# Neighbourhood attention with grid rows ordered by columns, and two heads at a time on halves of TensorE's array

## The chip, the cores and the metric

The kernel runs on one core of a Trainium2 chip. The time is the device time of one execution in microseconds (us), the median of several runs. A profile of one further execution gives the instructions of each engine: TensorE (PE, with its weight loads as PEld), VectorE (DVE), ScalarE (ACT), GpSimd (POOL) and SyncE (SP), the last of which mainly issues DMA transfers here.

## The reference, cut to what matters

Two transformer blocks in float32 over 512 tokens of width 1024. The first has neighbourhood attention beside a convolution branch, then a mixture of experts; the second has two kinds of causal attention and a layer of retrieved experts. Only the attention of the first block is changed. Its 512 tokens are a grid of 8 rows and 64 columns. A query sees all 8 rows, but only a window of 16 columns, and besides that 256 context keys:

```python
cq = jnp.arange(GRID_W)[:, None]                       # GRID_W = 64
ck = jnp.arange(GRID_W)[None, :]
c_start = jnp.clip(cq - WIN_COLS // 2, 0, GRID_W - WIN_COLS)   # WIN_COLS = 16
col_mask = (ck >= c_start) & (ck < c_start + WIN_COLS)
...
s_loc = einsum('bhqd,bhkd->bhqk', q_r, k_blk) * scale + bias   # bias from rpb by row and column distance
s_loc = jnp.where(band_mask, s_loc, NEG_INF)
s_ctx = einsum('bhqd,bhkd->bhqk', q_r, k_ctx) * scale
p = jax.nn.softmax(jnp.concatenate([s_loc, s_ctx], axis=-1), axis=-1)
return einsum('bhqk,bhkd->bhqd', p[..., :n_loc], v_blk) + einsum('bhqk,bhkd->bhqd', p[..., n_loc:], v_ctx)
```

## The kernel before

The program is one block of code per engine. Each engine runs its instructions in order, and semaphores (`wait_ge`, `then_inc`) tie the engines together; the order of the work is written out by hand. Almost every vector and scalar instruction goes through `link`, which also waits for its own end.

**Start.** SP loads four 2 MB slabs of `w_mod`, then the context and x (L620, L621). Rows are normalised, transposed on TensorE (L1884) and scaled into `hT` by ScalarE (L892, L895). Then TensorE makes the GLU inputs of the convolution (L1846), VectorE the product `u_pad` (L1377) and the depthwise convolution (L1382), while TensorE makes k, v and q: 18 projections, copied out by ScalarE (q at L917).

**Slabs.** All weights pass through a ring of six slots. SP issues slab n when slab n - 6 has been read (L618). Slabs 9 to 28 belong to five modulation jobs of four slabs each (the function `modulation`, L1861), slabs 29 to 34 to the merge.

**The attention loop** takes 32 units n, one head and 128 queries each. TensorE at step n: `scores(n)` (L1940: 512 local keys, L1941: 256 context keys, contraction over the 64 channels of the head), `transposes(n - 2)` (L1950: six 128x128 tiles), `weighted(n - 3)` (L1963: six products of 64x128 into one half of bank 6). VectorE adds the bias (with the window's mask in it) and takes the maximum (L1420), takes that of the context scores (L1422), joins them (L1423), then normalises unit n - 1 (L1406 to L1408). ScalarE makes the exponentials (L956, L958) and copies the transposed weights of unit n - 2 to SBUF (L944, L946), and at the end of a head its output (L952). Between the steps stand two sums of the convolution's layer norm (`conv_mean` L1903, `conv_var` L1909; on VectorE `conv_centre` and `conv_norm`), and at n = 6, 11, 16, 21 (`AT_JOB`) modulation jobs 1 to 4. A job writes four rows, on partitions 0, 32, 64 and 96; VectorE adds the bias to each (L1367), POOL stores them (L777). Job 0 runs among the projections.

**The bias.** POOL writes a table `skew_d`, 64 copies of each padded row of `rpb` (L768, four transfers, 3.9 MB), and reads from it for each head, with a skewed pattern in pieces of 256 bytes, a [128, 14, 64] bias (L795). These loads are spread over the loop, each behind the maxima of an earlier head.

**Merge.** For each of eight c TensorE computes two gates and two branch products (L1846), ScalarE the sigmoids (L978, L979), VectorE `mixT` (L1439 to L1441). Then `w_o`, the second norm and the experts.

## Time and profile before

| what | us |
|---|---|
| median of 3 runs | 3176.17 (3174.83 to 3188.65) |
| the profiled execution, whole | 3168.23 |
| its span, first to last instruction | 3166.5 |
| TensorE busy in the span | 2314.8 |
| VectorE busy | 1449.2 |
| ScalarE busy | 730.2 |

The span is what the views are dated in, from its first instruction. Busy time is a union over the instructions of an engine: matmuls overlap, so the mean duration of a record is longer than the pace at which records follow each other. A float32 product leaves two matmul records and a transpose one. Share of busy time says little by itself; what counts is which engine or transfer ends last at each place.

### The profile page before, as it was taken

The numbers are of one execution on the slowest core, as the hardware profiler recorded it, in microseconds if no ns is written. First come the engines' busy times: TensorE is split into PE (matmuls) and PEld (weight loads), VectorE is DVE, ScalarE is ACT, GpSimd is POOL, SyncE is SP. The second block draws the span as 40 slices with busy tenths as digits, with TensorE's granted clock in tenths as the row PEclk, the third lists the DMA queues.
The fourth block names the chain that finished last, engine by engine and source line by source line (L and its number), as shares of the span: only waits on it lengthen the run. The fifth ranks groups of instructions, "written<-read, shape, count | busy, mean of one in ns | idle before, by whom it ended". The sixth has DMA issues, their size and how long they took to land.

```text
span 3166.5 us, 29164 instructions
## 1 busy us (share of the span) xinstructions
PE 2314.8 (73%) x9846; PEld 1013.0 (32%) x9846; DVE 1449.2 (46%) x3427; ACT 730.2 (23%) x1764; POOL 615.8 (19%) x604
## 2 busy tenths in 40 slices
PE   2998999976787777299886887646775656565554
PEld 1444554442222222154465643312221111111110
DVE  1295431141000000300138766756777777777775
ACT  2004430011000000221225543312222322232222
POOL 1000100001000000100001222234444443444442
PEclk8999999977999899699788788777787777777777
DMA  7416833826999999621125777789999999999996
GB/s 258 167 54 217 289 115 109 258 98 263 405 405 404 406 406 402 215 102 53 54 73 205 282 292 278 291 338 394 416 418 421 421 421 421 421 412 421 422 421 278
DMA packets 218493, 928.24 MB, mean 293 GB/s; under 512 B 19385, under 2 KB 59384, under 8 KB 127486
## 3 DMA queue, kind: packets, MB, share of 16 engines
q0 software_dynamic: 80752, 558.26, 43.5%
q1 hardware_dynamic: 127824, 359.68, 30.7%
q10 hardware_dynamic: 9790, 8.73, 0.8%
q8 instruction: 66, 1.08, 0.1%
q14 instruction: 61, 0.50, 0.0%
HBM read 891.42 MB, written 35.18 MB: 293 GB/s over the span
## 4 chain that ended last, share of the span: by engine, by line
DMA 29%; PE 26%; DVE 12%; issue 5%; ACT 4%; POOL 1%; SPq 0%; DVEq 0%; POOLq 0%; ACTq 0%
DMA ring<-in_expert_pair,ids 14%; DMA ring<-in_w_exp_up 11%; PE bank L1846 7%; PE bank L2052 5%; PE bank L2370 4%; DVE ring L1795 4%; PE bank L1852 4%; DMA arena_v<-in_expert_pair,ids 2%; DMA pair_last<-in_expert_pair,ids 2%; PE bank L2383 1%; ACT arena_w L1248 1%; DMA ring<-in_w_exp_down 1%; POOL ring L852 1%; PE bank L2185 1%; PE bank L2186 1%
## 5 line engine op out<-in xcount | busy, mean ns | idle before, releaser
L2370 PE MATMUL bank<-ring,arena_w 128*32 128x512 f32 x1568 | 546.9, 818 | 356.0 <-ACT arena_w L1248 353.4
L852 POOL DMA_INDIRECT ring<-in_expert_pair,ids x392 | 423.4, 1080 | 1118.3 <-PE bank L2370 661.1
L1846 PE MATMUL bank<-arena_h,ring 128*128 128x512 f32 (+1 forms) x1024 | 373.2, 525 | 12.1 <-DMA ring<-in_w_in 10.0
L2052 PE MATMUL bank<-ring,arena_h 128*64 128x512 f32 x1056 | 278.7, 688 | 82.8 <-DMA ring<-in_w_exp_up 74.6
L2370 PEld LDWEIGHTS bank<-ring,arena_w 128*32 128x32 f32 x1568 | 94.3, 131 | 670.7 <-ACT arena_w L1248 502.1
L1795 DVE CUSTOM_DVE_ANT_0 ring<-ring,arena_h 128x1024 f32<-128x1024 f32 x203 | 245.8, 1226 | 114.6 <-DMA ring<-in_expert_pair,ids 82.6
L1795 DVE CUSTOM_DVE_ANT_0 ring<-ring 128x1024 f32<-128x1024 f32 x189 | 229.7, 1225 | 76.9 <-DMA ring<-in_expert_pair,ids 67.6
L1846 PEld LDWEIGHTS bank<-arena_h,ring 128*128 128x128 f32 x1024 | 178.8, 196 | 195.8 <-issue 192.8
L1541 DVE TENSOR_TENSOR arena_q<-arena_q,bank 128x256 f32<-128x256 f32 x32 | 13.5, 421 | 494.5 <-ACT arena_q L1016 494.5
L1246 ACT ACTIVATE arena_w<-arena_w 128x2 f32<-128x2 f32 (+1 forms) x224 | 45.4, 203 | 763.1 <-DVE arena_w L1795 762.9
L2052 PEld LDWEIGHTS bank<-ring,arena_h 128*64 128x64 f32 x1056 | 96.5, 157 | 263.5 <-issue 254.7
L2370 PE MATMUL bank<-pair_last,arena_w 128*32 128x512 f32 x200 | 134.4, 810 | 25.3 <-ACT arena_w L1248 25.3
L2065 PE MATMUL bank<-ring,arena_q 128*64 128x512 f32 x528 | 120.6, 598 | 19.8 <-DVE arena_q L1544 19.3
L1248 ACT ACTIVATE arena_w<-arena_w 128x32 f32<-128x32 f32 x512 | 132.9, 312 | 7.3
L2370 PE MATMUL bank<-arena_h,arena_w 128*32 128x512 f32 x140 | 96.2, 826 | 38.4 <-ACT arena_w L1248 38.4
L833 POOL DMA_INDIRECT arena_v<-ys_d,slot_i x8 | 8.0, 1004 | 574.4 <-SPq L682 564.2
L2370 PE MATMUL bank<-arena_v,arena_w 128*32 128x512 f32 x140 | 94.9, 816 | 33.0 <-ACT arena_w L1248 33.0
L1852 PE MATMUL bank<-ring,arena_h 128*128 128x512 f32 x224 | 100.7, 609 | 1.0 <-ACT arena_h L1192 0.8
L1382 DVE SCALAR_TENSOR_TENSOR arena_x<-arena_x,convc 128x512 f32<-128x512 f32 x120 | 90.2, 752 | 4.3
L1016 ACT ACTIVATE arena_q<-bank 128x256 f32<-128x256 f32 x32 | 12.3, 384 | 321.3 <-PE bank L2052 321.3
L1852 PE MATMUL bank<-ring,arena_q 128*128 128x512 f32 x176 | 78.0, 603 | 3.6 <-DVE arena_q L1441 3.6
L1439 DVE TENSOR_TENSOR arena_w<-bank,arena_w 128x512 f32<-128x512 f32 x8 | 5.5, 692 | 159.8 <-ACT arena_w L979 159.8
(465 smaller groups left out, 3248.5 us busy)
## 6 DMA issues: line engine op xcount, KB each, us to landing
ring<-in_w_exp_gate SPq DMA_DIRECT2D x33, 2048.0 KB, 19.8
ring<-in_w_exp_up SPq DMA_DIRECT2D x33, 2048.0 KB, 24.2
ring<-in_w_exp_down SPq DMA_DIRECT2D x33, 2048.0 KB, 25.0
ring<-in_w_in SPq DMA_DIRECT2D x15, 2048.0 KB, 22.8
ring<-in_w_mod SPq DMA_DIRECT2D x12, 2048.0 KB, 9.7
ring<-in_w_ada SPq DMA_DIRECT2D x12, 2048.0 KB, 18.3
xs_d<-zeros SPq DMA_DIRECT2D x1, 12032.0 KB, 69.4
arena_h<-xs_d SPq DMA_DIRECT2D x66, 128.0 KB, 23.2
```

The costliest lines, as they stand in the source:

```text
L852: pool.indirect_dma_start(pair[pair_of(m)], None, A["expert_pair_2"], bass.IndirectOffsetOnAxis(ap=ids[n % 2][:, r:r + 1], axis=0)).then_i ...
L1246: link(act.activation(gel[:, k0:k0 + count], dots[:, k0:k0 + count], ACT.Gelu))
L1248: act.activation(sel_q[:, n % 2, k, :], sel_q[:, n % 2, k, :], ACT.Copy, scale=gel[:, k:k + 1]).then_inc(sel_done, 1)
L1382: link(dve.scalar_tensor_tensor(out=conv[:, cc, :], in0=u_pad[:, cc, k:k + T], scalar=convc[:, cc, k:k + 1], in1=conv[:, cc, :], op0=ALU.m ...
L1795: dve.tensor_tensor_reduce(buf, buf, h2_q[r % 4], 1.0, 0.0, ALU.mult, ALU.add, dots[:, r:r + 1]).then_inc(dots_done, 1)
L1846: mm = pe.matmul(dst, w[:, c, at], rhs[:, c, :], start=(c == 0), stop=(c == chunks - 1))
L1852: mm = pe.matmul(dst, xT[:, c, t * P:(t + 1) * P], w[:, c, at], start=(c == 0), stop=(c == chunks - 1))
L2052: mm = pe.matmul(bank[2 + b][at, :].rearrange("p (g f) -> p g f", g=2), xbT[b][:, c, :], gu[:, :, c, 256 * half:256 * half + 256], start=( ...
L2065: mm = pe.matmul(bank[6 + b][CAP * j:CAP * j + CAP, :], hidT[b][:, k, CAP * half:CAP * half + CAP], slab(n)[:, half, k, 512 * j:512 * j + ...
L2185: pe.matmul(dst[:, 0:w], fqT[at, h // 2, t * P:(t + 1) * P], fkT[at, h // 2, 0:w], start=True, stop=False)
L2186: pe.matmul(dst[:, 0:w], ident[0:H, h:h + 1].broadcast_to([H, P]), fcumT[:, 0:w], start=False, stop=False)
L2370: mm = pe.matmul(bank[4 + 2 * (n // H % 2) + half][at, :], sel_q[:, n % 2, k0 + j, :], pair[pair_of(m + j)][:, D + 512 * half:D + 512 * ha ...
```

## The change

Tokens are held column by column in the first block's attention: position 8 c + r for grid column c and row r. A group of 128 queries (16 columns; q is rotated by 64 positions, that is 8 columns) then sees only 256 neighbouring keys, and the fourth group, made of the two edges, 128 each. x is loaded in that order by eight transfers, one per grid row. The convolution needs the order by rows, so `u_pad` is written, and the gates of the merge are written, through a permuted view (`by_columns`, `in_rows`).

The loop takes 16 units i (`PU`), each two heads and 128 queries. The heads of a pair sit on the two halves of the partitions, and `scores` and `weighted` alternate between them, on row halves and on column halves of the array. Local and context scores share one bank, so one maximum and one exponential per head do. VectorE adds the bias in the bank itself. The division of a unit's work is:

| per pair of heads and 128 queries | before | after |
|---|---|---|
| score products, columns | 4: 2 x 512, 2 x 256 | 4 x 256 |
| transposes | 12 | 8 (6 in every fourth) |
| weighted products of 128 columns | 12 | 8 |

The bias table becomes 23 copies of 120 rows of 48 floats, written in one transfer in pieces of 192 bytes; a pair's bias is read in pieces of 1536 bytes into `rpb_raw`, and VectorE makes the bias with the mask from it (`bias_of`). Jobs use a stationary operand of 32 equal columns in place of one, so that VectorE adds all 128 partitions in one instruction. The jobs move to steps 4, 8, 11 and 14 of 16. `probT` takes the space of `pair_last`. The core of the diff:

```diff
-        PROJ_JOB, AT_MEAN, AT_VAR, AT_JOB = 10, 1, 4, (6, 11, 16, 21)
+        PROJ_JOB, AT_MEAN, AT_VAR, AT_JOB = 10, 0, 2, (4, 8, 11, 14)
...
-                    sp.dma_start(xr, A["x"].rearrange("(t p) d -> p t d", p=P)).then_inc(x_in, 16)
+                    for r in range(ROWS):
+                        sp.dma_start(xr[r:P:ROWS, :, :], A["x"][r * GRID_W:(r + 1) * GRID_W, :].rearrange("(t c) d -> c t d", t=TT))\
+                            .then_inc(x_in, 16)
...
+            pool.dma_start(skew_d[:, :, :].rearrange("i n w -> n i w"),
+                           rpb_pad[0:H * RPB_R, :].unsqueeze(1).broadcast_to([H * RPB_R, COPIES, SKEW])).then_inc(skew_out, 16)
...
+            def bias_rows(hp):
+
+                if hp >= 1:
+                    pool.wait_ge(nmax_done, 8 * (hp - 1) + 1)
+                for e in range(2):
+                    at = skew.offset + ((2 * hp + e) * RPB_R + ROWS - 1) * SKEW + WIN - 1
+                    pool.dma_start(rpb_raw[:, e, :], bass.AP(skew.tensor, at, [[copy - 1, WIN], [copy - SKEW, ROWS], [1, ROWS * SKEW]]))                        .then_inc(bias_in[hp % 2], 16)
+
+            bias_rows(0)
+            store_rows(0)
+            bias_rows(1)
+            store_rows(1)
+            bias_rows(2)
+            store_rows(2)
+            bias_rows(3)
+            store_rows(3)
+            store_rows(4)
...
-                    link(act.activation(qT[:, m - 14, :], src[:, :], ACT.Copy, scale=HD ** -0.5), proj_out)
+                    link(act.activation(qT[:, m - 14, 0:T - 64], src[:, 64:T], ACT.Copy, scale=HD ** -0.5))
+                    link(act.activation(qT[:, m - 14, T - 64:T], src[:, 0:64], ACT.Copy, scale=HD ** -0.5), proj_out)
...
+            def exps(i):
+                w = LOC[i % TT] + CTX
+                for e in range(2):
+                    m = 2 * i + e
+                    act.wait_ge(nmax_done, m + 1)
+                    if m >= 6:
+                        act.wait_ge(pT_done, m - 5)
+                    link(act.activation(prob[m % 6][:, 0:w], bank[2 * (i % 2) + e][:, 0:w], ACT.Exp, bias=neg_max(m),
+                                        accum_out=ssum[:, 0, m:m + 1]), p_done)
+
+            def probs_out(i):
+                w = LOC[i % TT] + CTX
+                for e in range(2):
+                    m = 2 * i + e
+                    act.wait_ge(pT_done, m + 1)
+                    if m >= 4:
+                        act.wait_ge(o_done, m - 3)
+                    link(act.activation(probT[m % 4][:, 0:w // P, :], bank[4 + e][:, 0:w].rearrange("p (a b) -> p a b", b=P), ACT.Copy), pTa_out)
...
-                for j in range(4):
-                    at = slice(32 * j, 32 * j + 1)
-                    link(dve.tensor_tensor(mod_row[at, :], bank[7 if i else 0][at, :], mod_bias[i % 3][at, :], ALU.add), mod_rows)
+                dve.tensor_tensor(mod_row, bank[7 if i else 0][:, :], mod_bias[i % 3], ALU.add).then_inc(mod_rows, 4)
...
-                link(dve.tensor_tensor(u_pad[:, cc, PADC:PADC + T], bank[2 * (cc % 2)][:, :], sig[cc % 2], ALU.mult), u_done)
+                link(dve.tensor_tensor(in_rows(u_pad[:, cc, PADC:PADC + T]), by_columns(bank[2 * (cc % 2)][:, :]),
+                                       by_columns(sig[cc % 2]), ALU.mult), u_done)
...
+            def maxima(i):
+                w = LOC[i % TT]
+                for e in range(2):
+                    m = 2 * i + e
+                    s, b = bank[2 * (i % 2) + e], bias[:, e, 0:256] if w == 256 else bias[:, e, 256:384]
+                    dve.wait_ge(s_done, m + 1)
+                    link(dve.tensor_tensor(s[:, 0:w], s[:, 0:w], b, ALU.add))
+                    link(dve.tensor_reduce(neg_max(m), s[:, 0:w + CTX], AX, ALU.max, negate=True), nmax_done)
+
+            def normalise(i):
+
+                for e in range(2):
+                    m = 2 * i + e
+                    dve.wait_ge(p_done, m + 1)
+                    one = slice(m % 4, m % 4 + 1)
+                    link(dve.reciprocal(rinv[:, one], ssum[:, 0, m:m + 1]))
+                    p = prob[m % 6][:, 0:LOC[i % TT] + CTX]
+                    link(dve.tensor_scalar(p, p, rinv[:, one], None, ALU.mult), pn_done)
...
+                            rows, v = 32, cvec[:, vecs, c:c + 1].broadcast_to([P, 32])
...
+            def scores(i):
+                hp, u = i // TT, i % TT
+                if i >= 2:
+                    pe.wait_ge(p_done, 2 * i - 2)
+                keys = ((u * P, 2 * P, 0, P),) if u < TT - 1 else ((T - P, P, 0, 64), (0, P, 64, 64))
+                for k0, width, q0, queries in keys:
+                    for e in range(2):
+                        pe.matmul(bank[2 * (i % 2) + e][q0:q0 + queries, 0:width], qT[halves(e), hp, u * P + q0:u * P + q0 + queries],
+                                  kT[halves(e), hp, k0:k0 + width], start=True, stop=True)
+                for e in range(2):
+                    pe.matmul(bank[2 * (i % 2) + e][:, LOC[u]:LOC[u] + CTX], qT[halves(e), hp, u * P:(u + 1) * P],
+                              kcT[halves(e), hp, :], start=True, stop=True).then_inc(s_done, 1)
+
+            def transposes(i):
+                for e in range(2):
+                    m = 2 * i + e
+                    pe.wait_ge(pn_done, m + 1)
+                    if m >= 2:
+                        pe.wait_ge(pTa_out, m - 1)
...
+                for k, (v, chunk, q0, queries) in enumerate(terms):
+                    for e in range(2):
+                        at = slice((2 * hp + e) * HD, (2 * hp + e + 1) * HD)
+                        mm = pe.matmul(bank[6][halves(e), u * P + q0:u * P + q0 + queries], v[:, at],
+                                       probT[(2 * i + e) % 4][:, chunk, q0:q0 + queries], start=(k == 0), stop=(k == len(terms) - 1))
```

## Rows read from the trace of the kernel before

**Rows 1.** The page, part 2: busy tenths of TensorE in 40 equal slices of the span.
```profile
PE   2998999976787777299886887646775656565554
```

**Rows 2.** Timeline of PE, 225 to 460: start, duration, engine, line, operation.
```profile
277.51 4.34 PE L1909 MATMUL bank<-arena_x,mean_w 128*128 128x512 f32 x8
289.81 7.05 PE L1861 MATMUL bank<-ring,cvec 128*1 128x512 f32 x64
...
381.98 7.05 PE L1861 MATMUL bank<-ring,cvec 128*1 128x512 f32 x64
440.44 14.00 PE L1846 MATMUL bank<-arena_h,ring 128*128 128x512 f32 x32 [0.74 <-ACT arena_v L952]
```

**Rows 3.** By stretch, busy: PE, PEld, DVE, ACT, POOL; then PEclk, DMA share, GB/s.
```profile
254.00:440.40 186.40, 166.07 (x976) 99.91 (x976) 104.08 (x261) 93.59 (x215) 19.95 (x31) 0.94 0.74 252
440.40:636.00 195.60, 191.95 (x443) 84.76 (x444) 20.75 (x30) 13.38 (x21) 4.01 (x7) 0.99 0.55 165
...
138.20:254.40 116.20, 115.57 (x349) 55.25 (x347) 96.23 (x129) 9.83 (x18) 2.01 (x4) 1.00 0.21 73
```

**Rows 4.** Timeline of one step, 398 to 414: PE and its weight loads.
```profile
403.84 0.88 PE L1950 MATMUL bank<-ident,spare 128*128 128x128 f32 x6
...
404.64 1.28 PEld L1963 LDWEIGHTS bank<-arena_w,arena_v 128*64 128x64 f32 x12 [0.17 <-issue]
...
406.10 1.12 PE L1940 MATMUL bank<-arena_q 64*128 64x512 f32 x2
...
407.06 0.59 PE L1941 MATMUL bank<-arena_v,arena_q 64*128 64x256 f32 x2
```

**Rows 5.** Chain that ended last: start, duration; expert products on 64-column halves.
```profile
757.22 6.89 PE bank L2052 x32
```

**Rows 6.** Groups by form, 254 to 441: busy us, mean ns, idle before.
```profile
L1408 DVE TENSOR_SCALAR arena_w<-arena_w,rinv 128x768 f32<-128x768 f32 x22 | 14.0, 635 | 0.8
L1422 DVE TENSOR_REDUCE smx<-bank 128x1 f32<-128x256 f32 x32 | 13.6, 424 | 1.1
...
L1407 DVE RECIPROCAL rinv<-rinv 128x1 f32<-128x1 f32 x32 | 5.3, 164 | 1.1
...
L1313 DVE RECIPROCAL arena_x<-arena_x 128x512 f32<-128x512 f32 x1 | 3.4, 3352 | 0.0
```

**Rows 7.** Groups by form, 0 to 1050: a 512-wide pass of VectorE from a bank.
```profile
L1439 DVE TENSOR_TENSOR arena_w<-bank,arena_w 128x512 f32<-128x512 f32 x8 | 5.5, 692 | 159.8 <-ACT arena_w L979 159.8
```

**Rows 8.** Line L618: three slab loads issued from 325 to 330, time to landing.
```profile
L618 SPq DMA_DIRECT2D ring<-in_w_ada x3: 540/667/3872, 327.8 to 329.1; - x3
DMA to landing us min/median/max: 9.8/14.6/19.3
```

**Rows 9.** Timeline of the start, by engine.
```profile
78.72 21.45 PE L1846 MATMUL bank<-arena_h,ring 128*128 128x512 f32 x43 [10.01 <-DMA ring<-in_w_in]
...
53.92 3.43 POOL L768 DMA_DIRECT2D skew_d<-arena_w  x3 [1.71 <-DMA arena_w<-in_rpb]
...
43.55 1.06 ACT L883 ACTIVATE arena_q<-arena_v 128x1024 f32<-128x1024 f32 x1 [24.67 <-DMA arena_x<-in_x]
...
64.69 6.46 ACT L895 ACTIVATE arena_h<-bank,mcol,acol 128x512 f32<-128x512 f32 x8
```

**Rows 10.** Line L618: three slab loads issued from 52 to 56, time to landing.
```profile
L618 SPq DMA_DIRECT2D ring<-in_w_in x3: 551/669/1631, 53.0 to 54.3; - x3
DMA to landing us min/median/max: 14.8/25.0/32.1
```

**Rows 11.** DMA, 84 to 100: rate in 40 slices; bias loads, size and landing.
```profile
GB/s 415 394 353 379 389 394 404 399 410 399 389 399 384 394 379 399 404 328 215 225 236 230 230 164 230 246 230 236 251 251 236 215 215 231 312 389 389 384 384 389
...
arena_w<-skew_d POOLq DMA_DIRECT2D x4, 224.0 KB, 8.5
```

**Rows 12.** By stretch of 3 us, columns as in rows 3.
```profile
303.00:306.00 3.00, 0.93 (x7) 0.79 (x8) 2.86 (x6) 1.83 (x6) 2.55 (x6) 1.00 1.00 354
306.00:309.00 3.00, 3.00 (x13) 2.51 (x13) 1.79 (x5) 2.26 (x6) 1.54 (x2) 0.52 1.05 393
```

242 lines of the change are left out of this document (101 added, 141 removed).

## The prediction

> **What bounds the kernel now.** Start from the page [rows 1]: slices 2 to 8 (79 to 633 us) hold TensorE at 80% and more, and the change touches only this front part, before the experts. Next the timeline of TensorE [rows 2] dates the stages: the attention loop ends at 440.4, where the merge of the branches begins. Inside it stand four modulation jobs of 7.05 us, the first at 289.8 and the last at 382.0, so 30.7 us apart, and two convolution sums of about 4 us (one stands in rows 2). The loop begins at 254.4, where the projections end [rows 3]. The table of stretches [rows 3] says what limits the loop: of 186.4 us TensorE is busy 166.1, VectorE 104.1, ScalarE 93.6, and the DMA engines 0.74 of the time. So the loop is TensorE's; VectorE and the weight stream are the next two floors. One steady step [rows 4] shows the order: transposes 403.84, weighted sums 404.64, scores 406.10 and 407.06, which end at 407.65. With the waits between about 4 us a step, in 32 steps.
>
> The merge waits for all of the loop, and after it TensorE is busy 191.95 of 195.6 us [rows 3]. The expert weights are loaded into slots that the merge frees, so the stages behind move with it. I carry a gain at 440 us through one for one.
>
> **Scores.** Before: per step a 64x512 and a 64x256 product, two records each; 1.56 us from 406.10 to the end at 407.65 [rows 4]; for a pair of heads 3.1. After: per pair of heads and 128 queries four products of 256 columns, eight records. A 512-column record costs 0.44 us back to back (14.00 us for 32) [rows 2], so a 256-column one 0.22. One behind another: 8 x 0.22 = 1.75. Two at a time: 0.9, with gaps 1.1. No row shows row halves at work together (the two heads there write two banks). The nearest rows are column pieces: the expert product on 64-column halves takes 6.89 us for 32 records, 0.215 each, and the modulation 7.05 us for 64, 0.11 each [rows 5, 2], against 0.44 whole [rows 2]. I take 1.1 and keep 1.75.
>
> **Transposes.** Six in 0.88 us, 0.145 each [rows 4]. From 12 to 8 per pair (6 in every fourth unit): 1.16 us.
>
> **Weighted sums.** 12 records of 128 columns in 1.46 us (404.64 to 406.10), 0.12 each [rows 4]; before, all of a head go to one half. Per pair from 24 to 16 alternating records: 2.0 us one behind another, 1.1 side by side. Here [rows 5] speaks directly for the halves, so 1.1.
>
> TensorE's step is 1.1 + 1.16 + 1.1 = 3.4 us. The Trainium skill ("TensorEngine Tiling (Array Packing)", Key Properties) says that a change of tiling mode drains TensorE, and each step has three changes. The trace shows 0.17 us at such a point (0.17 <-issue [rows 4]). By the page such drains stay, but there are 16 steps with them in place of 32; priced at the row it is 0.5 us a step, and 3.9 in place of 3.4.
>
> **VectorE.** Per head: an add of 256 from and to a bank (no row writes to a bank; the nearest pass from one is 424 ns for 256 [rows 6]), a maximum over 512 (692 for a 512-wide pass [rows 7]), a reciprocal of 0.164 and a scaling of 512 (0.635 for 768 [rows 6]; 0.42 in proportion, 0.49 with a fixed part). With 0.05 between links: 3.9 us per pair, 3.2 in every fourth unit, mean 3.7. Bounds: the bank write at 0.3 to twice 0.42, so 3.6 to 4.7. ScalarE, busy 93.6 us in the old loop [rows 3], has four passes of 512 per pair (two exponentials, two copies) where it had eight of 512 or 256, so it is not the bound. VectorE sets the step, about 3.9 us. Besides it keeps what it had: centring, four passes of 0.69; normalisation, a reciprocal of 3.35 and eight passes, about 9; and bias preparations, four of about 1.5 [rows 6, 7]. The rows of a job fall from four passes to one.
>
> **Jobs.** The same 64 products in 7.05 us; weight loads of 32 columns in place of 1. The expert products have loads of 64 columns and keep the full pace for two halves [rows 5], so such loads lie under products. Cost 0 to 1 us each; I take 0.
>
> **The weight stream.** This becomes the floor. Each job uses four 2 MB slabs and frees their four slots; the next job needs the first two of the batch issued then. After the second job the loads go out from 327.8 on and land 9.8, 14.6 and 19.3 us later [rows 8]: about 4.7 us of lead and 5.1 a slab, unless an earlier batch is still running. Job to job is thus at least 7.05 + 14.6 = 21.7 us, near the bandwidth floor of 4 x 5.1 = 20.4. Before, the interval was 30.7, and the stream had pauses (share 0.74 [rows 3]).
>
> **The loop, added up.** To job 1 (step 4): five steps, the two sums of 8 us, and the waits between sums and VectorE's centring and variance: about 25 us. By then job 1 has its slabs: three are issued as the projections end and land by 4.7 + 3 x 5.1 = 20 us. Job 1 to 2, four steps: VectorE has normalisation 9, about 4 x 3.9 of steps, a bias 1.5 and the rows 0.7: 27 us. Jobs 2 to 3 and 3 to 4, three steps each: 7 + 3 x 3.9 is 19, less than the 21.7 of the stream, so 22 each. After job 4: 7 us, then the remaining step and three draining ones, about 14 us; the merge's first four slabs, two of which are issued only after job 4, need 14.6. So 22. Sum 25 + 27 + 22 + 22 + 22 = 118, plus 2 for a dip of the clock: **120 us in place of 186, 66 less**.
>
> **The start.** TensorE stands still for 10 us until 78.7, when its second GLU slab lands (issued 53.6, 25.0 us) [rows 9, 10]. That slab shares the engines with the bias table's copies, three of 960 KB issued from 53.9 [rows 9]. After, the table is 2760 pieces of 192 bytes, 0.53 MB. Pieces of 256 bytes can be priced: from 91 to 97 us four loads of 224 KB (3584 pieces) pull the rate from about 395 to about 230 GB/s [rows 11]; own bytes and loss make some 1.9 MB, about 4.9 us, 1.4 ns a piece. So 2760 cost 3.8 us: the slab at 53.6 + 14.6 + 3.8 = 72. The inputs of the product are ready at 71.2 (64.69 + 6.46) [rows 9]. The stage starts at 72.2, **6.5 us earlier**, and stays TensorE-bound to 254 [rows 3], so the gain passes. Bounds 9 and -8 (writes five times as dear). Loading x in eight strided pieces in place of one: the bytes are the same, ScalarE began on them at 43.55 [rows 9], and a delay has 0.9 us of cover by the slab, which would land at 72. 0, at worst 3.
>
> **Covered.** The GLU's strided write has 14 us of products per piece (16 products of two records of 0.44). Two copies for one in q and at the heads' end: 0.2 each. The merge's strided sigmoids and product stand beside 24 us of products per turn (195.6 in eight [rows 3]); only the last turn shows, 0 to 2. POOL: each bias load now stands in front of a store of rows and is issued when the pair before has been read; none comes late. TensorE's in-order wait for a job's slabs now has scores queued behind it; VectorE waits for these, and that is in the 22s.
>
> **Sum.** 66 + 6.5 = 72.5 less than the 3168.2 us of the profiled execution: 3095.7. The runs' median is 8 us higher, so 3104.
>
> **Rivals.** (1) The halves do not run together (the change does not do what it says, as to time). For: no row has row halves in fp32. Against: [rows 5]. TensorE's step is 1.75 + 1.16 + 2.0 + 0.5 = 5.4: 16 x 5.4 + 28 + 8 + 8 = 130 us, 10 more: 3114. If only the rows fail, 3108. (2) The clock. With TensorE busy 0.93 of 3 us, the granted clock in the next 3 us is 0.52, the level of 1.2 GHz [rows 12]. The new loop has many short waits. With half of it at 1.2 GHz TensorE's steps average 5.1 and some jobs take 14: 15 us more, 3119; all of it, 31 more, 3135. The Trainium skill ("TensorE: Matmul & The Clock Gate", Loop structure matters more than you think) says that gaps between bursts let the clock fall; the trace agrees [rows 12], but the 0.94 over the loop says how seldom so far [rows 3]. (3) A larger gain: steps of 3.6, clean stream, 110 us and 9 at the start: 85 less, 3091. (4) Slower than before: the 192-byte writes. They share the engines with the GLU slabs; each ns a piece delays these by 2.8 us, so above 72.5 / 2.76 + 1.4 = 28 ns the whole gain is gone; at 40 the stage starts at 53.6 + 14.6 + 110 = 178, 106 after the 72.2 of the forecast: 3210. Against: 1.4 ns for the like read.
>
> **How the numbers follow.** Forecast 0.55, (1) 0.15, (2) 0.17, (3) 0.10, (4) 0.03. The range 3088 to 3138 takes in the first four. Half a percent (about what a measurement here tells from no change) is 16 us: faster 0.94, same 0.03, slower 0.03.
>
> **What would show it.** Right: the four jobs some 22 to 27 us apart, each ending a wait for a slab; TensorE's idle time ended by DMA in jobs 3 and 4; the expert-like 0.11 to 0.15 us per record in scores and sums; GLU products from about 72. Wrong: score records not overlapping, VectorE's add well over 0.42, a clock near 0.5 over long stretches, a late x, or a merge that begins well away from 367.

## The result, and the profile after

| what | us |
|---|---|
| median of before, 4 runs | 3175.5 (3169.76 to 3188.65) |
| median of after, 4 runs | 3129.05 (3124.04 to 3138.84) |
| ratio, with its 95% interval | 0.9852 (0.9812 to 0.9892) |
| the profiled execution of after, whole and span | 3138.84, 3137.0 |

The kernel is 46 us faster, 1.5%. The forecast was 72 us and 3104; the time lies in the range of 3088 to 3138, 25 us above the forecast. A second series of the same kernel (`a1_after_again`, below) gave 3128.31 and a ratio of 0.9811 (0.9765 to 0.9858). The profiled execution of after is the slowest of its four, so its span is only 29.5 us shorter than that of before (3166.5).

The timeline of TensorE of after, to be read against [rows 2] and [rows 9]. Columns: start, duration, engine, line, operation, tiles and number of records, and in brackets the idle time before it and what ended that. L1897 is a modulation job, L1944 the convolution's second sum, L1878 at 379.90 the first product of the merge. In the loop L1979 and L1982 are scores, L1992 transposes, L2006 weighted sums.

```profile
75.62 9.61 PE L1878 MATMUL bank<-arena_h,ring 128*128 128x512 f32 x18 [2.54 <-ACT arena_h L913]
...
251.60 3.70 PE L1938 MATMUL bank<-arena_x,mean_w 128*128 128x512 f32 x8
...
265.90 5.75 PE L1944 MATMUL bank<-arena_x,mean_w 128*128 128x512 f32 x8 [4.47 <-ACT arena_x L946]
...
278.32 7.07 PE L1897 MATMUL bank<-ring,cvec 128*32 128x512 f32 x64
285.32 0.70 PE L1979 MATMUL bank<-arena_q 64*128 64x256 f32 x4
285.86 0.60 PE L1982 MATMUL bank<-arena_v,arena_q 64*128 64x256 f32 x4
286.39 0.88 PE L1992 MATMUL bank<-ident,arena_w 128*128 128x128 f32 x6
287.19 1.09 PE L2006 MATMUL bank<-pair_last,arena_v 128*64 128x128 f32 x16
288.22 0.70 PE L1979 MATMUL bank<-arena_q 64*128 64x256 f32 x4
...
297.39 1.94 PE L1992 MATMUL bank<-ident,arena_w 128*128 128x128 f32 x8 [8.04 <-ACT pair_last L976]
...
307.48 7.07 PE L1897 MATMUL bank<-ring,cvec 128*32 128x512 f32 x64
...
331.02 8.77 PE L1897 MATMUL bank<-ring,cvec 128*32 128x512 f32 x64 [3.21 <-DMA ring<-in_w_ada]
...
355.28 8.77 PE L1897 MATMUL bank<-ring,cvec 128*32 128x512 f32 x64 [4.13 <-DMA ring<-in_w_ada]
...
379.90 15.36 PE L1878 MATMUL bank<-arena_h,ring 128*128 128x512 f32 x32 [6.58 <-DMA ring<-in_w_conv_out]
```

The merge starts at 379.90 in place of 440.44, so 60.5 us earlier. The mechanism of the forecast is in the last three rows: job 3, job 4 and the merge each stand behind a wait for a slab. Before job 2 there is no such wait; there TensorE waits 8.04 us for ScalarE's copy of earlier transposes. This copy stands behind the convolution's SiLU (L955) and the exponentials, and SiLU stands behind VectorE's normalisation. ScalarE's timeline of that stretch:

```profile
289.17 1.28 ACT L955 ACT_TABLE_LOAD   x1 [5.12 <-DVE arena_x L1421]
290.46 3.35 ACT L955 ACTIVATE arena_x<-arena_x,convc 128x512 f32<-128x512 f32 x4
293.84 1.28 ACT L966 ACT_TABLE_LOAD   x1
295.13 0.69 ACT L966 ACTIVATE arena_w<-bank,smx 128x512 f32<-128x512 f32 x1
...
296.75 1.01 ACT L976 ACTIVATE pair_last<-bank 128x384 f32<-128x384 f32 x2
```

VectorE's first maximum of the step is ready at 292.46 (291.77 + 0.69 in its timeline), and ScalarE's exponential on it starts only at 295.13, behind SiLU and its two table loads. A part of TensorE's step is read by starts: scores 285.32 to 286.39, 1.07 us; weighted sums 287.19 to 288.22, 1.03 us.

By stretch, the first row for the loop, the second for GLU and projections, as in [rows 3] (PE, PEld, DVE, ACT, POOL busy, then PEclk, DMA share, GB/s):

```profile
250.40:379.80 129.40, 93.72 (x792) 52.38 (x792) 74.07 (x155) 58.32 (x119) 14.27 (x28) 0.88 0.93 329
75.60:250.40 174.80, 173.97 (x480) 81.50 (x480) 98.98 (x132) 14.18 (x27) 2.10 (x4) 0.99 0.24 85
```

The loop has shrunk from 186.4 to 129.4 us. TensorE was busy 0.89 of it and is now busy 0.72; the DMA share has risen from 0.74 to 0.93, VectorE's part from 0.56 to 0.57. From job 2 on the loop belongs to the weight stream now. VectorE's groups by form in the loop (busy, mean ns, idle before), to be set against [rows 6, 7]:

```profile
L1440 DVE TENSOR_REDUCE smx<-bank 128x1 f32<-128x512 f32 x24 | 16.6, 691 | 0.8
L1450 DVE TENSOR_SCALAR arena_w<-arena_w,rinv 128x512 f32<-128x512 f32 x24 | 11.8, 492 | 0.8
L1439 DVE TENSOR_TENSOR bank<-bank,arena_w 128x256 f32<-128x256 f32 x24 | 10.3, 431 | 33.5 <-PE bank L1982 33.0
L1448 DVE RECIPROCAL rinv<-ssum 128x1 f32<-128x1 f32 x32 | 5.2, 163 | 1.1
```

Four durations, four hits: 0.691 for 0.69, 0.492 for 0.49, 0.431 for 0.42, 0.163 for 0.164. The 33.0 us of idle time ahead of the add are spent waiting for scores, so VectorE isn't the bound of the whole loop either.

### The profile page after: what moved, and what is told of

It reads as the page before. It is cut to its first block, busy times and chain, and to the rows that moved or that the text cites. A ratio compares the mean times of both kernels' runs of the same rounds, so it can differ in the third digit from the quotient of the medians.

```text
span 3137.0 us, 28550 instructions
## 1 busy us (share of the span) xinstructions
PE 2262.7 (72%) x9662; PEld 971.0 (31%) x9662; DVE 1419.5 (45%) x3317; ACT 703.2 (22%) x1672; POOL 603.3 (19%) x593
## 4 chain that ended last, share of the span: by engine, by line
DMA 32%; PE 27%; DVE 11%; issue 4%; ACT 4%; POOL 1%; SPq 0%; DVEq 0%; POOLq 0%; ACTq 0%
DMA ring<-in_expert_pair,ids 17%; DMA ring<-in_w_exp_up 11%; PE bank L1878 7%; PE bank L2097 5%; PE bank L2415 5%; DVE ring L1827 4%; PE bank L1884 3%; DMA arena_v<-in_expert_pair,ids 1%; POOL ring L870 1%; PE bank L2428 1%; ACT arena_w L1274 1%; DMA pair_last<-in_expert_pair,ids 1%; PE bank L2230 1%; DMA ring<-in_w_exp_down 1%; PE bank L2231 1%
## 5 line engine op out<-in xcount | busy, mean ns | idle before, releaser
L1878 PE MATMUL bank<-arena_h,ring 128*128 128x512 f32 (+1 forms) x1024 | 372.5, 524 | 10.5 <-DMA ring<-in_w_conv_out 6.6
L2097 PE MATMUL bank<-ring,arena_h 128*64 128x512 f32 x1056 | 282.7, 696 | 91.6 <-DMA ring<-in_w_exp_up 81.2
L1878 PEld LDWEIGHTS bank<-arena_h,ring 128*128 128x128 f32 x1024 | 178.6, 196 | 193.4 <-issue 188.7
L1878 PE MATMUL bank<-arena_q,ring 128*128 128x384 f32 x224 | 81.0, 524 | 0.0
## 6 DMA issues: line engine op xcount, KB each, us to landing
ring<-in_w_exp_up SPq DMA_DIRECT2D x33, 2048.0 KB, 24.8
```

The costliest lines, as they stand in the source:

```text
L1878: mm = pe.matmul(dst, w[:, c, at], rhs[:, c, :], start=(c == 0), stop=(c == chunks - 1))
L2097: mm = pe.matmul(bank[2 + b][at, :].rearrange("p (g f) -> p g f", g=2), xbT[b][:, c, :], gu[:, :, c, 256 * half:256 * half + 256], start=( ...
```

## Where 26 us of the forecast went

The sum forecast a merge 72.5 us earlier, and the rest carried through. Here is each stretch in several traces, dated by the first products of merge and experts, the last gate or up product of the experts, and the span. `before`, `b1` and `b2` have the attention of before; in `b2` x comes in eight transfers.

| stretch, us | before | b1 | b2 | after | a1 | e6 |
|---|---|---|---|---|---|---|
| start to GLU | 78.7 | 80.3 | 82.3 | 75.6 | 73.2 | 73.5 |
| start to merge | 440.4 | 442.1 | 442.3 | 379.9 | 378.2 | 371.8 |
| merge to experts | 302.1 | 302.1 | 300.5 | 305.6 | 305.5 | 304.4 |
| experts | 544.1 | 537.3 | 536.1 | 557.4 | 550.5 | 547.2 |
| experts' end to the end | 1879.9 | 1886.7 | 1896.6 | 1894.1 | 1895.3 | 1896.8 |

Before the merge 12.0 us are missing: 3.4 at the start (3.1 gained of 6.5) and 9.3 in the loop (56.7 of 66), less 0.7 that the projections gave. Behind it the stages take longer: 3.6 us from merge to experts and 13 in the experts by the two profiled executions, and in the last row 14 us more, though that row varies by 17 among the traces with the attention of before alone. Of these stages the change touches only the merge. Its 3.6 us can be read in the two timelines. The first products take 15.36 us in place of 14.00. At the end of the merge the two sigmoids through the permuted view take 1.03 us each for 0.60 and VectorE's permuted product 1.02 for 0.69, so that `w_o` starts 8.40 us after the start of the last branch products in place of 7.20. And `w_o` itself takes 57.99 us for 56.90, at a granted clock of 0.52 in its first 6 us where before has 0.72. The experiments take up the rest in turn.

## Experiments

### The two kernels again

`a1_after_again` is after, `b1_before_again` is before, unchanged, to know how far the dates of one trace can be trusted.

> The changed kernel once more, unchanged. In its first trace the merge began at 379.9 us, 60.5 us before that of the kernel before, but the lead shrank to 43.7 us over the expert stage (683.7 to 1248.5 us, 375 GB/s, against 740.6 to 1292.2 at 384 GB/s) and to 29.5 us at the end. Theory 'executions differ there': this trace shows the merge again at 380 within 1 us, and an expert stage of another length, anywhere from 551 to 565 us. Theory 'the change costs something in the expert stage' (data lies elsewhere in memory, since the bias table is smaller): again 564 to 566 us. Time 3129 within 8 us in both.

> The kernel before once more, unchanged, for a second trace. Its first trace had GLU at 78.7, the merge at 440.4, an expert stage of 544.1 us (first to last product) and 1456.6 us from the first to the last sum of retrieved experts; four traces of changed kernels have 548 to 557 and 1459 to 1473. Theory 'executions differ by that much, and the first trace of before was a short one': this trace has 548 to 557 or 1460 to 1473 in at least one of the two, with GLU and merge within 1.5 us of the first. Theory 'the change lengthens these later stages': 544 and 1457 again, within 2 us.

a1: 3128.31 us (3106.86 to 3131.35). Its GLU starts at 73.15, 2.5 us before that of after, its merge at 378.17, and its experts last 550.5 us for 557.4. b1: 3170.02 us in a single run, GLU at 80.28, merge at 442.07, experts 537.3 us for 544.1. In a1 the merge is 1.7 us off, a little more than the 1 us of the first theory, and the experts differ by 7 us, as it said. In b1 they differ by as much, but downwards, so neither of its two theories fits. So a date of the front has 2 to 2.5 us of play, the length of the experts about 7, and the last stage up to 17 (b2). The difference at the merge, 60.5 and 63.9 us in the two pairs, is far above it; a difference of 5 us in the last stage isn't. Whole times of single runs tell little: those of before, over all series, lie between 3161 and 3197 us, those of after between 3107 and 3139.

### Smaller slabs for the later jobs

If the stream sets the loop, then less of it must give back the three waits. `e3_half_slabs` leaves out half of each slab of jobs 1 to 4 and of the merge, so it computes something else:

```diff
-                sp.dma_start(slab(n), src).then_inc(slab_in[n % RING], 16)
+                if N_JOB + 4 <= n < N_WO:
+                    sp.dma_start(slab(n)[:, 0:shape[0] // 2, :], src[:, 0:shape[0] // 2, :]).then_inc(slab_in[n % RING], 16)
+                else:
+                    sp.dma_start(slab(n), src).then_inc(slab_in[n % RING], 16)
```

> Left out: half of the weights of modulation jobs 1 to 4 and of the merge are not loaded (every such slab is 1 MB in place of 2), the instructions of the engines are the same; the result is not the reference's. Theory 'from job 2 on the weight stream sets the pace': the waits for DMA before jobs 3 and 4 (3.2 and 4.1 us) and before the merge (6.6) go, the two jobs take 7.07 in place of 8.77 us since no wait lowers the clock, intervals between jobs 2, 3 and 4 are 19 to 20 in place of 23.5 and 24.3, and the merge begins at 363 to 367 in place of 379.9. Rival 'the waits are only a sign, the engines' chain is as long': the merge moves by less than 3 us.

It took 3102.86 us in a single run. Its timeline of TensorE, the same three places:

```profile
325.70 7.19 PE L1900 MATMUL bank<-ring,cvec 128*32 128x512 f32 x64
...
344.19 7.07 PE L1900 MATMUL bank<-ring,cvec 128*32 128x512 f32 x64
...
361.50 14.00 PE L1881 MATMUL bank<-arena_h,ring 128*128 128x512 f32 x32 [0.98 <-ACT arena_v L985]
```

No wait for a transfer is left, and the merge starts at 361.50, 18.4 us earlier than in after. Of these, 2.0 us were there at job 1 already (276.28 for 278.32); 16.4 arise behind job 2, where the loads differ. The first theory had forecast 363 to 367. The jobs are back at 7.07 to 7.19 us and the merge's first products at 14.00, where after has 8.77 and 15.36. That is the clock. The stretches of job 1 and job 3 of after, and of job 3 of e3:

```profile
278.30:285.40 7.10, 7.10 (x68) 2.06 (x66) 6.79 (x10) 4.48 (x8) 0.00 (x0) 1.00 0.44 160
331.00:339.80 8.80, 8.78 (x66) 2.88 (x66) 1.15 (x3) 0.00 (x0) 0.00 (x0) 0.81 1.05 385
```
```profile
325.70:332.90 7.20, 7.20 (x68) 1.96 (x66) 1.79 (x3) 0.43 (x1) 0.00 (x0) 0.98 0.16 46
```

The mean granted clock is 1.00 in job 1, 0.81 in job 3, behind a wait of 3.21 us for its slab, and 0.98 in the same job without that wait. So a wait for a slab costs twice: its own length, and 1.7 us in the 7 us job behind it. Over all traces with the new attention the jobs behind such a wait take 8.37 to 9.85 us, so 1.3 to 2.8 more, and the waits before them are 2.3 to 5.4 us; the longer wait isn't always the dearer one. The dip comes behind the wait and isn't left over from the step before: in both kernels the step ahead of job 3 runs at the lower clock (granted 0.57 from 324.2 to 327.8 in after; its sixteen weighted records take 1.98 us in both), but only where a wait follows does the job lose time too. The Trainium skill ("TensorE: Matmul & The Clock Gate", Loop structure matters more than you think) says that products behind a DMA wait run cold; the trace agrees.

Here is the chain from job to job in after: 314.5 (job 2 ends) + 16.5 = 331.0; 339.8 + 15.5 = 355.3; 364.1 + 15.8 = 379.9. The forecast had 14.6 for the landing and 7.05 for each job. So 21.7 became 23.5, 24.3 and 24.6, which is 6.4 us against the three 22s. In the first of these gaps two bias loads of 192 KB share the DMA engines with the slabs, from 322.5 on; in the second there is none.

### Heads in turn

`e2_heads_in_turn` puts all of head 0's products before those of head 1, for scores and weighted sums. If alternation is what makes the halves run together, the products of the two heads should follow one another, and if TensorE sets the loop, it should lengthen.

```diff
-                for k0, width, q0, queries in keys:
-                    for e in range(2):
+                for e in range(2):
+                    for k0, width, q0, queries in keys:
...
-                for k, (v, chunk, q0, queries) in enumerate(terms):
-                    for e in range(2):
+                for e in range(2):
+                    for k, (v, chunk, q0, queries) in enumerate(terms):
```

> Same products, but first all of one head, then all of the other, in scores and in weighted sums, so that neighbouring instructions use the same half of the array. Theory 'the halves work together only if the instructions alternate': sixteen weighted records take 1.9 to 2.0 us in place of 1.05, the eight score records 1.7 in place of 1.15, TensorE's step 5 in place of 3.4; but the slab stream and VectorE set the pace, so the merge begins only 2 to 10 us later (382 to 390). Rival 'the time of the step is that of TensorE': 16 steps x 1.5 = 24 us later, at 404. Rival 'order does not matter': 1.05 and 1.15 as now.

It took 3123.23 us in a single run, and the merge began at 381.16. Its timeline of TensorE:

```profile
285.33 0.71 PE L1979 MATMUL bank<-arena_q 64*128 64x256 f32 x4
285.87 0.60 PE L1981 MATMUL bank<-arena_v,arena_q 64*128 64x256 f32 x4
286.41 0.87 PE L1991 MATMUL bank<-ident,arena_w 128*128 128x128 f32 x6
287.21 1.58 PE L2005 MATMUL bank<-pair_last,arena_v 128*64 128x128 f32 x16
288.72 0.71 PE L1979 MATMUL bank<-arena_q 64*128 64x256 f32 x4
...
299.93 0.44 PE L1979 MATMUL bank<-arena_q 64*64 64x128 f32 x4
300.29 0.70 PE L1981 MATMUL bank<-arena_v,arena_q 64*128 64x256 f32 x2
300.92 0.44 PE L1979 MATMUL bank<-arena_q 64*64 64x128 f32 x4
301.28 0.70 PE L1981 MATMUL bank<-arena_v,arena_q 64*128 64x256 f32 x2
301.91 1.09 PE L1991 MATMUL bank<-ident,arena_w 128*128 128x128 f32 x8
```

Three things are to be seen. The weighted sums, on column halves, take 1.51 us in place of 1.03 (287.21 to 288.72). The scores of a plain unit, on row halves, stay at 1.08 us (285.33 to 286.41): their single records still start two by two, 13 ns apart in place of 7, though the program has head 0's four records first. In every fourth unit, whose local products are on quarters, the heads do stand one behind the other: 1.98 us (299.93 to 301.91), where after needs 1.01. That the halves can run together is thus shown for both kinds: with the products in turn the same records take 1.5 and 2 times as long. None of the three theories holds for all of them, and why the order tells in some places and not in others isn't settled.

TensorE has some 12 us more work here (16 x 0.48 and 4 x 0.97), and the merge starts 1.3 us later than in after, 3.0 later than in a1. From GLU to merge it is 306.9 us, where they have 304.3 and 305.0. TensorE doesn't set the loop.

### The normalisation, a piece per step

TensorE's longest wait, 8.04 us after job 1, ends behind VectorE's normalisation, which is done in one go while two heads' scores stand ready, and behind ScalarE's SiLU on its result. `e4_norm_spread` spreads the normalisation over five steps and moves SiLU behind the last, so it changes both at once. ScalarE's part of the edit, then VectorE's:

```diff
-                if i == AT_VAR + 2:
+                if i == AT_VAR + 3 + CC:
                     conv_silu()
...
-                if i == AT_VAR + 2:
-                    conv_norm()
+                if AT_VAR + 2 <= i <= AT_VAR + 2 + CC:
+                    conv_norm(i - AT_VAR - 3)
```

> VectorE's normalisation of the convolution is spread: at i = 4 only the inverse root, then one of its four passes at each of i = 5 to 8, and ScalarE's four SiLU passes move from i = 4 to i = 9, so that copies of transposed weights no longer stand behind them. Theory 'TensorE's 8.0 us wait between jobs 1 and 2 is ScalarE standing in front of SiLU, behind VectorE's 9 us of normalisation': the interval from job 1 to job 2 falls from 29.2 to 22 to 25 us and, since jobs 3, 4 and the merge follow the slab stream, the merge comes 4 to 7 us earlier (372 to 376). Rival 'the slab stream takes it all back': job 2 earlier, but job 3, 4 and merge at the same dates within 1.5 us.

It took 3120.03 us in a single run. Job 1 to job 2 is 25.9 us (277.12 to 303.04), where after has 29.2; from GLU to merge 301.1, where after and a1 have 304.3 and 305.0. The longest wait for ScalarE falls from 8.0 to 5.7 us. What is left of it stands behind the inverse root, which VectorE still does in one go: ScalarE's next exponential starts at 288.44, when the first maximum is ready. Behind job 2 the intervals are 24.3, 23.2 and 24.8 us, as they were. Job 3 now waits for no slab and takes 7.07 us, but job 4 and the merge still wait, 4.8 and 6.8 us. So what is won before job 2 stands, and the stream gives nothing more. How much of it is VectorE's passes and how much ScalarE's SiLU wasn't told apart.

### x: eight transfers, four, one

ScalarE takes up x when all of it has landed. In before that was at 43.55 [rows 9]. In after:

```profile
49.10 1.06 ACT L901 ACTIVATE arena_q<-arena_v 128x1024 f32<-128x1024 f32 x1 [28.28 <-DMA arena_x<-in_x]
```

`e7_x_plain` loads x as before, by one transfer in natural order, with the instructions of after, so that its attention computes something else. `e1_x_four_loads` loads the new order by four transfers, one for each tile of 128 partitions. `b2_x_eight` is before with its natural order loaded by eight transfers of 16 partitions. `e8_x_side_by_side` is after with each grid row's tokens on 16 neighbouring partitions in place of every eighth, which again leaves another order. The edit of e1:

```diff
-                    for r in range(ROWS):
-                        sp.dma_start(xr[r:P:ROWS, :, :], A["x"][r * GRID_W:(r + 1) * GRID_W, :].rearrange("(t c) d -> c t d", t=TT))\
-                            .then_inc(x_in, 16)
+                    for t in range(TT):
+                        sp.dma_start(xr[:, t, :], A["x"].rearrange("(r t c) d -> t c r d", r=ROWS, t=TT)[t]).then_inc(x_in, 16)
```

> x loaded by the one plain transfer of the kernel before (tokens in their natural order, so the attention computes something else; the instructions of all engines are the same; the result is not the reference's). Theory 'the gather by columns slows the load of x': ScalarE begins on x at 43 to 44.5 in place of 46.2 to 49.1, GLU at 71.5 to 72.5, merge 374 to 376. Rival 'the load of x varies from run to run and the order does nothing': it begins at 46 to 49, as in the runs so far.

> x loaded in the same order by four transfers of 128 partitions, in place of eight that write 16 partitions each. Theory 'writes to every eighth partition run at half pace' (213 GB/s from 36 to 46 us, at full busy share of the DMA engines, against 386 before): the rate stays near 400, ScalarE begins on x at about 43.5 to 44 in place of 49.1, the GLU products at 70 to 72 in place of 75.6, and the loop and the merge 3.5 to 5 us earlier (merge 375 to 376.5). Rival 'it is the row-wise gather from memory, whatever partitions it goes to': x arrives at 49 again and nothing moves. Time 3125 by the first, 3129 by the rival.

> The kernel before, all as it was, but x comes in eight transfers of 16 neighbouring partitions each, in the natural order of the rows. It answers two things. (a) Load of x: one plain transfer starts ScalarE at 43.55 to 44.11; gathered loads in four or eight transfers at 46.2 to 50.5, whatever partitions they go to. Theory 'the gathered rows of memory are the cause': 43.5 to 45 here, at 390 GB/s and more from 36 to 40 us. Rival 'the number of transfers': 46 or later, near 200 GB/s. (b) Later stages: the two traces of before have an expert stage of 544.1 and 537.3 us and 2410 us from its first product to the last sum of retrieved experts; ten with the change's attention have 547 to 557 and 2419 to 2438. Theory 'the extra transfers on SP's queue are what slows the later streams': 547 or more and 2419 or more here. Rival 'they are not': 537 to 545 and 2410 again.

> As the changed kernel, eight transfers of x from the same rows of memory, but each to 16 neighbouring partitions in place of every eighth (tokens end in another order, so the attention computes something else and the result is not the reference's). Plain x starts ScalarE at 43.55 to 44.11, the gathered ones at 46.2 to 49.1. Theory 'partitions eight apart are slow to write': it starts at 43.5 to 45. Rival 'the rows in memory, or the number of transfers, are the cause' (four transfers over all 128 partitions were slow too, 46.2): 46 to 49.

| kernel | transfers, order | GB/s, 36 to 40 | ScalarE's first on x | GLU starts | time |
|---|---|---|---|---|---|
| before | 1, natural | 386 | 43.55 | 78.72 | |
| e7 | 1, natural | 401 | 43.62 | 71.95 | 3123.75 |
| e1 | 4 of 128 partitions, new | 239 | 46.23 | 72.72 | 3130.40 (ratio 0.9834) |
| after, a1 | 8 of 16, new | 214, 197 | 49.10, 46.65 | 75.62, 73.15 | 3129.05, 3128.31 |
| e2, e3, e4, e9 | 8 of 16, new | 147 to 221 | 47.73 to 49.24 | 74.25 to 76.00 | |
| e8 | 8 of 16 side by side, new | 198 | 50.45 | 76.97 | 3165.56 |
| b2 | 8 of 16, natural | 147 | 52.86 | 82.34 | 3177.21 |

The rows of the stretch 36 to 40 us, after first, then b2, columns as in [rows 3]:

```profile
36.00:40.00 4.00, 4.00 (x20) 0.61 (x16) 0.00 (x0) 0.00 (x0) 0.00 (x0) 1.00 1.02 214
```
```profile
36.00:40.00 4.00, 3.38 (x20) 0.69 (x24) 0.00 (x0) 0.00 (x0) 0.00 (x0) 1.00 1.03 147
```

The share is 1.02 and 1.03: the 16 DMA engines are fully taken and move about half of what they do with one transfer. b2 settles what it is about the eight transfers: its order is natural, its transfers are narrow, and ScalarE starts latest of all. So the cut into eight transfers of 16 partitions is enough by itself; neither the gathering of rows nor the stride over partitions is needed. Whether it is their number or their width wasn't told apart, nor, for e1's four full-width transfers, cut and gathering. e1 itself shows no gain: its 46.23 stands beside 46.65 in a1 and 46.37 in `e5_more_table_writes`, which load by eight. The Trainium skill ("DMA: Bandwidth & Descriptors", Rules for kernel authors) asks for 128 partitions and at least 1 MiB a transfer where bandwidth matters; after has 16 partitions and 256 KB, and the trace agrees with the rule. The prediction argued from the bytes alone.

e7 also dates the start. Its timeline of TensorE:

```profile
71.95 13.54 PE L1876 MATMUL bank<-arena_h,ring 128*128 128x512 f32 x31 [3.47 <-DMA ring<-in_w_in]
```

With x as before, the GLU starts at 71.95 behind its slab, where the forecast had 72.2 with the slab at 72. So the term for the bias table was right, and the 3.7 us between 71.95 and 75.62 are the price of x; in a1 it is 1.2. (e8's experts take 592 us. Its tokens are in an order of their own; why its experts are longer is open, and its whole time says nothing about x.)

### Table writes put back

`e5_more_table_writes` adds three writes of 960 KB beside the slabs, as the table of before had them:

```diff
+            for h in range(0, 6, 2):
+                at = slice(h * RPB_R, (h + 2) * RPB_R)
+                pool.dma_start(extra_d[at, :, :], ident[at, :].unsqueeze(1).broadcast_to([2 * RPB_R, GRID_W, P])).then_inc(extra_out, 16)
```

> As the changed kernel, with three more transfers of 960 KB from SBUF to memory in front of the bias table, the volume that the old table had there. Theory 'the old table's writes delayed the second GLU slab': GLU products at 78 to 80 in place of 73.2 to 75.6, and the merge as much later. Rival 'the gain at the start has another source': GLU stays below 76.

```profile
76.57 8.93 PE L1884 MATMUL bank<-arena_h,ring 128*128 128x512 f32 x14 [5.75 <-DMA ring<-in_w_in]
```

The wait for the slab is back, 5.75 us of it, and the GLU starts at 76.57, between the 78 of the theory and the 76 of its rival; the whole took 3135.5 us in a single run. Against e7's slab at 71.95 the writes cost 4.6 us. Before's start was 78.72, so the sign is as expected and the size less.

### The experts: is it the table's place?

The experts last 536.1 to 544.1 us in the three traces with the attention of before, and 547.2 to 557.4 in ten with the new one (e8 left out): means 539.2 and 550.2, with no overlap. They are bound by the expert weights: by the pages, TensorE waits 74.6 us in before and 81.2 in after ahead of their products for a slab of them. The stretch 800 to 1000 us of before, after and b2, columns as above:

```profile
800.00:1000.00 200.00, 160.18 (x648) 58.98 (x648) 10.15 (x24) 18.35 (x35) 0.00 (x0) 0.91 1.02 404
```
```profile
800.00:1000.00 200.00, 156.91 (x636) 57.45 (x632) 10.14 (x24) 18.35 (x35) 0.00 (x0) 0.90 1.02 397
```
```profile
800.00:1000.00 200.00, 157.67 (x652) 58.80 (x650) 10.14 (x24) 18.93 (x36) 0.00 (x0) 0.92 1.02 409
```

The share is 1.02 in all three; the rate is 404, 397 and 409 GB/s. From 1000 to 1200 us it is 405, 393 and 411. Over all traces but e8's the first stretch has 404 to 409 with the attention of before and 397 to 404 with the new one, the second 405 to 411 and 393 to 401. The change alters one allocation in the chip's main memory, the table, from 3.9 to 0.53 MB, and so perhaps the place of what comes behind. `e9_table_room` is after with the table in an allocation of the old size:

```diff
-        skew_d = dram("skew_d", [COPIES, H * RPB_R, SKEW])
+        room = dram("skew_d", [H * RPB_R, GRID_W, 128])[:, :, :]
+        skew_d = bass.AP(room.tensor, room.offset, [[H * RPB_R * SKEW, COPIES], [SKEW, H * RPB_R], [1, SKEW]])
```

> As the changed kernel, but the bias table keeps the 3.9 MB of memory it had before (most of it unused), so that whatever is allocated behind it has its old place. Two traces of the kernel before have an expert stage of 544.1 and 537.3 us at 404 to 410 GB/s; eight traces with the small table have 548 to 557 at 393 to 403. Theory 'place in memory': the expert stage is back at 537 to 545 us, and the time 8 to 15 us below the changed kernel's 3129 (3114 to 3121). Rival 'something else in the change, or when it happens': 548 to 557 again and 3123 to 3132.

It took 3133.41 us (3129.46 to 3135.65), ratio 0.9844 (0.9785 to 0.9902), its experts 547.5 us at 404 and 400 GB/s. It is no faster than after, so the theory of the table's size and place falls. Nor is it the number of transfers at the start (b2: 536.1) or the order of x (e7, with x as before: 552.1). What remains was not tried: the rearranged buffers in SBUF, and the experts' starting some 60 us earlier. The cause of these 11 us stays open.

### Three edits together

`e6_best` joins e1's loads of x, e4's normalisation and jobs 2 to 4 one step earlier each, so that the stream can start sooner. The third edit:

```diff
-        PROJ_JOB, AT_MEAN, AT_VAR, AT_JOB = 10, 0, 2, (4, 8, 11, 14)
+        PROJ_JOB, AT_MEAN, AT_VAR, AT_JOB = 10, 0, 2, (4, 7, 10, 13)
```

> Three edits together: x by four transfers, the normalisation spread, and the jobs at steps 4, 7, 10 and 13 in place of 4, 8, 11 and 14. Theory 'from job 1 on, the slab stream is the floor (22 to 24 us a job)': job 1 near 274, jobs 2 to 4 at intervals of 23 to 25, merge at 368 to 372, 8 to 11 us before the changed kernel's 378 to 380, median 3117 to 3121. Rival 'no further gain, the steps between the jobs now miss at the end': merge at 374 to 376 as with the spread alone.

It took 3117.5 us (3115.09 to 3121.93), ratio 0.9791 (0.9733 to 0.9849). e9, which is after but for the table's room, ran beside it at 3129.46 to 3135.65; the two don't overlap, and e6 is 16 us faster by the medians. It is less sure against after itself: one of a1's runs took 3106.86. Its merge starts at 371.75, 8.8 us before that of e9, and the profiled executions of the two differ by 9.9 us; the rest of the 16 is in runs without a trace. TensorE's waits from 250 to 380 us (total, number, longest), after first, then e6:

```profile
PE bank L1992 <- ACT pair_last L976: 9.0, 2, 8.0
PE bank L1992 <- DVE arena_w L1450: 8.1, 7, 2.4
PE bank L1897 <- DMA ring<-in_w_ada: 7.3, 2, 4.1
PE bank L1878 <- DMA ring<-in_w_conv_out: 6.6, 1, 6.6
```
```profile
PE bank L1992 <- DVE arena_w L1450: 11.3, 7, 2.9
PE bank L1897 <- DMA ring<-in_w_ada: 7.7, 2, 5.4
PE bank L1992 <- ACT pair_last L975: 5.4, 3, 3.1
...
PE bank L1878 <- ACT arena_v L981: 1.0, 1, 1.0
```

The wait of 6.6 us for the merge's slabs is gone, since the last job stands a step further ahead of it, though the interval from job 4 to the merge is still 24.3 us. ScalarE's and VectorE's part of the waits is 16.7 in place of 17.1. The two waits before jobs stay, and these jobs take 8.37 and 9.49 us.

## Why the prediction was right, and where it was not

- **What bounds the loop afterwards: right behind job 2.** Jobs 3 and 4 and the merge end waits for slabs; with half slabs the three waits are gone, and 16.4 us behind job 2 with them. Jobs 1 and 2 end no such wait, though the forecast's sign said each would.
- **TensorE's step: right, a little too dear.** Scores 1.07 for 1.1, eight transposes 1.02 for 1.16 (302.77 less 301.75 in the timeline), weighted sums 1.03 for 1.1. These are taken from start to start, so any gap at a change of mode is in them: 3.12 us, with no sign of the 0.5 that the forecast priced as an addition. Row halves do run together in fp32, which no row of before could show, so rival (1) didn't occur. e2 gives TensorE 12 of the 32 us that rival (1) would have added, and 2 to 3 us of them arrive at the merge; what all of it would have cost no run shows. The sign "0.11 to 0.15 us per record" fits the scores (1.07 for eight) and not the sums (1.03 for sixteen, 0.064), for which the forecast's own 1.1 was 0.07.
- **VectorE's step: right.** The four passes and gaps of a unit are 3.88 us (291.30 to 295.18 in its timeline), for 3.9.
- **Weight loads of 32 columns for the jobs: right**, 7.07 for 7.05 us at full clock.
- **The five intervals of the loop: each too short; here lies the step that failed.** 27.8 for 25 (projections' end to job 1), 29.2 for 27, 23.5, 24.3 and 24.6 for 22 each; the 2 for the clock covers a part. The sum is 129.4 for 120. The last three were sized at 7.05 + 14.6; measured are jobs of 8.77 behind a wait, and 15.5 to 16.5 us from a job's end to the next start. The clock stood in the sum as one flat term of 2 us, while dips stand behind waits, those among them that the forecast itself put before jobs 3 and 4 and the merge: rival (2) in small, at 1.7 us for each 7 us job. There is such a dip in the first interval too: the convolution's second sum, behind a wait of 4.47 us, takes 5.75 us where the first takes 3.70. Against rows of the same products at full clock, eight rows of the loop took some 9 us more. In the second interval the forecast named VectorE alone as the bound and took ScalarE for none; TensorE's 8.04 us there ended behind ScalarE, where SiLU and two table loads, from 289.17 to 295.13, stood in no term; they held up an exponential whose maximum was ready at 292.46.
- **The start: the table right, x wrong.** "0, at worst 3" for x in eight pieces: ScalarE's first pass is 5.5 us later in after and 3.1 in a1, and the GLU 3.7 and 1.2 us behind e7's. The term was taken from the bytes alone. The 6.5 us of the start lie inside what the pairs of traces give, 3.1 by before and after, 7.1 by b1 and a1.
- **Covered: nearly.** The merge's last turn shows 1.2 us, for 0 to 2. "None comes late" is wrong for the bias loads: VectorE waits 1.26 and 3.02 us for two of them (at 306.43 and 330.36). The second ends in the stretch in which TensorE waits for job 3's slab.
- **"I carry a gain at 440 us through one for one": wrong.** Of 60.5 us at the merge 46 arrive at the end. 3.6 go before the experts: 1.4 in the products at the lower clock behind the merge's wait (15.36 for 14.00), 1.2 in the permuted last turn and 1.1 in `w_o` at a lower clock. e3 and e6, which have no such wait, take 303.0 and 304.4 us from merge to experts, for the 302.1 of before; the permuted turn is in both, the dip in `w_o` in e6. About 11 go in the experts, by the means of the two groups of traces; no term of the forecast stands for this, and its cause is open. The last stages don't tell the two kinds apart.
- **The rivals.** Clock: happened in part. Larger gain: no. Writes of 192 bytes that cost 28 ns or more each: no, as e7's start of 71.95 excludes them.

By size, then: 12 us before the merge, about 14 behind it. The merge begins 12 us after the 367 that the forecast gave as its sign, and more than half of what is missing lies in stages for which it had no term. So the mechanism of the loop was right from job 2 on, but that the whole time still fell into the range is owed to the range's width of 50 us, and in part to luck.

## What to carry to other kernels

When TensorE's work in a stage is halved, price the stage at its next floor, and put the clock on each wait that this floor makes: the job behind a 3 us wait took 8.77 us in place of 7.07. Look, too, at the engine behind the one that sets a stretch: ScalarE's SiLU and table loads stood between VectorE's work and TensorE's. Don't count a rearranged load by its bytes: cut into eight transfers of 16 partitions it ran at about half the rate. And what is won early in a kernel is an upper bound for the end when hundreds of microseconds behind it run on the memory's rate: compare the untouched stages in more than one trace of each kernel before the loss or gain is explained.

## What the hardware showed that I had not expected

- Eight transfers of 16 partitions and 256 KB each took the DMA engines' whole time (share 1.01 to 1.06 from 36 to 40 us) at 147 to 221 GB/s, where one transfer of 2 MB moved at 386 to 401.
- Two heads' scores on row halves ran together with the heads' products in turn (1.08 us a pair), while column halves lost half of their overlap (1.51 for 1.03) and the units with products on quarters all of it (1.98 for 1.01).
- A job of 64 products took 8.37 to 9.85 us behind a wait of 2.3 to 5.4 us and 7.07 without one, at a granted clock of 0.81 and 1.00 in the two that were read.
- The same expert stage, with the same code and a DMA share of 1.02, took 536 to 544 us in one set of kernels and 547 to 557 in another, at 404 to 409 against 397 to 404 GB/s in the same stretch. What in the layout or the timing does this wasn't found.
